# The first third of the adaLN product in two halves by output feature, with block 0 of the input projection begun on the first half; the squares of x summed along rows on ACT

## The chip, the cores and the metric

The kernel runs on one core of a Trainium2 chip. The metric is device time in microseconds (us). A core has a matrix engine (PE), a vector engine (DVE), a scalar engine (ACT), GpSimd (POOL), a sequencer that here only issues transfers (SP), and 16 DMA engines that all queues share.

## The reference, cut to what matters

One layer of a decoder trunk, for 256 prompt tokens and 8 sample tokens (264 in all, T), D = 1024, all float32:

```
mod = silu(c) @ w_ada + b_ada                  # 9 rows of c; (1024 x 6144), six parts of 1024: sh1 sc1 gt1 sh2 sc2 gt2
h   = rmsnorm(x, norm1_g) * (1 + sc1) + sh1    # x * rsqrt(mean(x*x) + eps) per token
proj = h @ w_in                                # (1024 x 9216)
...                                            # pooling and retention mixers, gates, w_out, x = x + gt1 * mix
...                                            # second modulated norm, router, top-4 of 32 experts, final norm
```

Everything in `proj` needs `h`, and `h` needs columns 0 to 2047 of `mod` (sh1 and sc1). The other 4096 columns are needed much later.

## The kernel before, in words

**Layout.** Inside the core x is held turned: `xT` and `hT` are [128 partitions, 8 chunks k of the feature, 264 tokens]. The rows of x (`xtok`, three tiles of tokens) are turned by PE, and ACT copies each chunk out of PSUM.

**Weights through a ring.** Three buffers of 2 MiB, `ring[0..2]`, take weights in the order of the list `order`: twelve loads of w_ada (`("ada", n)`) and eighteen blocks of 512 columns of w_in (`("in", p)`). SP issues a load when the last user of its buffer is done (`fetch`). The first four ada loads (`ADA_FIRST`) hold two chunks k each, of the columns 0 to 2047; the other eight hold one chunk k each of columns 2048 to 6143, and stand between the blocks of w_in. The order is ada 0 to 3, in 0, ada 4, in 1, ada 5, in 2, and so on. A buffer is used again by the third load after it.

**PE.** It turns c and x, multiplies ada 0 and 1 with c, sums the squares of x (`sum_squares`: ones times the squares that ACT writes chunk by chunk), turns the pooling state of the samples (`old_inputs_turned`), multiplies ada 2 and 3, and turns the 9 rows of sh1 and sc1 back into columns (`ada_columns(0)`). Only then can block 0 start. From there on it goes block, ada, block, ada.

**DVE and ACT.** DVE turns the sum into 1/rms for every token on all partitions (`norm`: scale, ACT's square root, a reciprocal of 128x264), multiplies `xT` by it, copies the adaLN rows out of PSUM (`stage_rows`), adds the bias (`take_columns`) and makes `scale1`. ACT then scales and shifts eight chunks of `hT` (`modulate`), and each one lets PE's first matmuls of block 0 go (`h_ready`).

**POOL** waits until all eight chunks of `hT` are done, and then loads the rest of the constants (1.96 MB) and eight rows of bias on a queue of its own. ACT loads the pooling state (`spool`, 0.48 MB) at the start on its queue.

**Later stages** are a retention stage with states streamed in and out, the up and out projections, and the experts, whose weights (32 times 12 MiB) pass through six buffers.

## Time and profile before

| | us |
|---|---|
| median of 3 runs (1546.3 to 1547.55) | 1547.12 |
| the profiled execution | 1545.43 |
| its span, first to last instruction | 1543.6 |
| PE busy | 1274.3 (83%) |
| share of PE and of DMA in the chain that ended last | 56% and 40% |
| first matmul of block 0 starts | 37.35 |
| first matmul of block 1 starts | 55.21 |

The profile shows one execution. Busy time of an engine is a sum over the program; the chain of waits follows the work that ended last, back from the end, and says of each piece whether it was an engine at work or a transfer. An arrow in a row names what the engine was waiting for. fp32 matmuls appear as two records each. "128*32" means that 32 columns of weights were loaded, so four such matmuls lie side by side in the array.

### The profile page before, as it was taken

To read this page: it belongs to the slowest core of one execution; us is meant where nothing else is said; L and a number is where in the kernel's file an instruction comes from. 1 tells how busy PE (TensorE), PEld (TensorE's weight loads), DVE (VectorE), ACT (ScalarE), POOL (GpSimd) and SP (SyncE) were. 2 spreads that over 40 slices of the span, in tenths; PEclk is the share of its full clock that TensorE was granted. 3 is DMA by queue.
4 is the path that set the end of the run, shared out by engine and by line. 5 is a ranking of instruction groups with operands and counts; after the bars stand their busy time and mean duration, and the time that the engine had idled before them with its cause. 6 is when DMAs were issued, how large, how long until landed. Compare 5 with 4: busy or idle time off the path is not lost.

```text
span 1543.6 us, 27740 instructions
## 1 busy us (share of the span) xinstructions
PE 1274.3 (83%) x10968; PEld 701.2 (45%) x10969; DVE 348.2 (23%) x747; ACT 308.1 (20%) x636; POOL 180.4 (12%) x296
## 2 busy tenths in 40 slices
PE   6999999998999889999965499576978666964594
PEld 3777887666887634444422134232433222421141
DVE  1023114332511432222211122111221112211123
ACT  3000122443100212222211022111212111211123
POOL 0240100110360001111100001000100000000000
PEclk9999999999999889999987689787989878887697
DMA  9876724999454576799999999999999999999994
GB/s 365 305 277 236 272 90 172 374 393 357 150 192 175 207 313 263 282 427 423 418 426 423 416 405 424 425 428 426 413 426 412 427 421 419 409 430 425 423 412 177
DMA packets 76666, 534.76 MB, mean 346 GB/s; under 512 B 6356, under 2 KB 7468, under 8 KB 49777
## 3 DMA queue, kind: packets, MB, share of 16 engines
q1 hardware_dynamic: 67330, 503.47, 79.7%
q0 software_dynamic: 8912, 29.90, 5.9%
q10 hardware_dynamic: 391, 0.93, 0.2%
q8 instruction: 23, 0.38, 0.1%
q14 instruction: 10, 0.08, 0.0%
HBM read 508.74 MB, written 28.09 MB: 348 GB/s over the span
## 4 chain that ended last, share of the span: by engine, by line
PE 56%; DMA 40%; DVE 2%; SPq 1%; issue 1%; ACT 0%; DVEq 0%; POOL 0%; POOLq 0%; ACTq 0%
DMA ring<-in_w_expert_in_dram 21%; PE ps L749 14%; PE ps L899 14%; PE ps L923 9%; DMA moe_ring<-in_w_expert_out_dram 8%; DMA moe_ring<-in_w_expert_in_dram 4%; DMA vslot<-in_state_ret_dram 3%; PE ps L504 2%; PE ps L868 2%; PE ps L776 2%; PE ps L822 2%; PE ps L784 2%; PE ps L791 2%; DMA ring<-in_w_ada_dram 1%; PE ps L551 1%; DMA ring<-in_w_in_dram 1%
## 5 line engine op out<-in xcount | busy, mean ns | idle before, releaser
L899 PE MATMUL ps<-ring,xgT 128*32 128x512 f32 x2352 | 323.5, 673 | 178.4 <-DMA ring<-in_w_expert_in_dram 177.7
L749 PE MATMUL ps<-hT,ring 128*128 128x264 f32 x1152 | 267.6, 390 | 3.0 <-DMA ring<-in_w_in_dram 3.0
L749 PEld LDWEIGHTS ps<-hT,ring 128*128 128x128 f32 x1152 | 218.2, 191 | 56.8 <-issue 19.5
L899 PEld LDWEIGHTS ps<-ring,xgT 128*32 128x32 f32 x2352 | 66.6, 117 | 320.1 <-DMA ring<-in_w_expert_in_dram 184.9
L923 PE MATMUL ps<-moe_ring,actT 128*32 128x256 f32 x3136 | 182.7, 381 | 3.2 <-DMA moe_ring<-in_w_expert_out_dram 2.4
L1135 ACT ACTIVATE ostage<-ps,slots_w 32x256 f32<-32x256 f32 x196 | 91.5, 467 | 288.0 <-PE ps L923 286.2
L1483 DVE COPY xg<-ps 128x256 f32<-128x256 f32 x49 | 20.8, 425 | 546.8 <-PE ps L868 546.8
L923 PEld LDWEIGHTS ps<-moe_ring,actT 128*32 128x32 f32 x3136 | 99.5, 111 | 86.6 <-issue 19.8
L899 PE MATMUL ps<-moe_ring,xgT 128*32 128x512 f32 x784 | 93.6, 595 | 19.6 <-DMA moe_ring<-in_w_expert_in_dram 19.6
L868 PE MATMUL ps<-rows,picked 128*32 128x256 f32 (+1 forms) x1200 | 81.8, 386 | 0.0
L1127 ACT COPY actT<-ps 128x256 f32<-128x256 f32 x49 | 18.3, 373 | 306.8 <-PE ps L504 306.8
L1493 DVE TENSOR_SCALAR glu_g<-ps 64x512 f32<-64x512 f32 x49 | 33.5, 683 | 178.1 <-PE ps L899 178.1
L1632 POOL CAST bias_sel<-ct 96x32 bf16 x49 | 10.4, 211 | 537.7 <-PE ps L899 294.9
L1642 POOL DMA_INDIRECT moe_rows<-ostage,slot_u x49 | 65.7, 1341 | 35.4 <-issue 34.5
L1118 ACT COPY lin<-ps 64x512 f32<-64x512 f32 x49 | 28.5, 582 | 176.8 <-PE ps L899 176.8
L899 PEld LDWEIGHTS ps<-moe_ring,xgT 128*32 128x32 f32 x784 | 23.3, 109 | 84.8 <-issue 44.0
L504 PEld LDWEIGHTS ps<-ct,act 64*128 64x128 f32 x196 | 27.2, 210 | 53.9 <-issue 53.9
L868 PEld LDWEIGHTS ps<-rows,picked 128*32 128x32 f32 (+1 forms) x1200 | 33.4, 108 | 38.5 <-issue 21.2
L1474 DVE TENSOR_SCALAR picked<-ct,item_base,rankm 128x128 f32<-128x128 f32 x147 | 42.2, 344 | 36.5 <-issue 36.5
L1637 POOL COPY slot_u<-slots_u 128x1 uint32 x49 | 9.0, 184 | 310.9 <-ACT ostage L1135 310.9
L1041 ACT ACTIVATE outer<-ps,projT 128x512 f32<-128x512 f32 x64 | 38.7, 696 | 7.8 <-DVE vslot L1354 7.8
L876 PEld LDWEIGHTS ps<-slot_v,picked 128*128 128x128 f32 x300 | 38.0, 194 | 3.2 <-issue 3.2
(276 smaller groups left out, 1112.5 us busy)
## 6 DMA issues: line engine op xcount, KB each, us to landing
ring<-in_w_expert_in_dram SPq DMA_DIRECT2D x96, 2048.0 KB, 11.9
moe_ring<-in_w_expert_out_dram SPq DMA_DIRECT2D x64, 2048.0 KB, 12.2
moe_ring<-in_w_expert_in_dram SPq DMA_DIRECT2D x32, 2048.0 KB
ring<-in_w_in_dram SPq DMA_DIRECT2D x18, 2048.0 KB, 11.7
ring<-in_w_ada_dram SPq DMA_DIRECT2D x12, 2048.0 KB, 8.7
ring<-in_state_ret_dram SPq DMA_DIRECT2D x8, 1024.0 KB, 11.1
vslot<-in_state_ret_dram SPq DMA_DIRECT2D x8, 1024.0 KB, 14.3
out_dram<-ring POOLq DMA_DIRECT2D x8, 1024.0 KB, 8.7
```

The lines of the kernel that those rows point to most:

```text
L504: return nc.tensor.transpose(out, in_, ident[0:in_.shape[0], 0:in_.shape[0]])
L749: mm = nc.tensor.matmul(ps[:, j, 0:T], ring[s][:, k, j * P:(j + 1) * P], hT[:, k, :], start=(k == 0), stop=(k == KC - 1))
L776: mm = nc.tensor.matmul(ps[:, ba, 0:T], a[:, k, m * P:(m + 1) * P], projT[:, Q0 + k, :], start=(k == 0), stop=(k == KC - 1))
L868: mm = nc.tensor.matmul(side(6, g)[:, 0:QUARTER], picked[0:n, t, 0:SLOTS], rows[0:n, t, g * QUARTER:(g + 1) * QUARTER], start=(t == 0), st ...
L876: mm = nc.tensor.matmul(ps[:, 5, 0:2], picked[:, t, :], values, start=(t == 0), stop=(t == 2))
L899: mm = nc.tensor.matmul(side(0, g), xgT[:, a, j * SLOTS:(j + 1) * SLOTS], w[:, a, g * COL:(g + 1) * COL], start=False, stop=(j == 3 and a ...
L923: mm = nc.tensor.matmul(side(2, g)[:, 0:QUARTER], actT[:, a, h * SLOTS:(h + 1) * SLOTS], w[:, a, g * QUARTER:(g + 1) * QUARTER], start=Fal ...
L1041: nc.scalar.activation(outer[:, n % 2, c, :], ps[:, 4 + n % 2, :], ACT.Copy, scale=projT[:, K0 + 2 * h + c, TP + b:TP + b + 1]).then_inc(o ...
L1135: mv = nc.scalar.activation(ostage[:, g * QUARTER:(g + 1) * QUARTER], ps[side, 2, 0:QUARTER], ACT.Copy, scale=slots_w[side, bass.ds(q, 1)])
L1474: ts(picked[:, t, :], const("slot"), item_base[:, bass.ds(q, 1)], rankm[:, t, bass.ds(e, 1)], ALU.add, ALU.is_equal).then_inc(picked_ready, 1)
L1493: ts(glu_g[:], ps[0:2 * SLOTS, 0, :], LIMIT, None, ALU.min).then_inc(glu_ready, 1)
L1642: pool.indirect_dma_start(out=moe_rows, out_offset=bass.IndirectOffsetOnAxis(ap=slot_u[0:SLOTS, 0:1], axis=0), in_=ostage[:], in_offset=No ...
```

## The change

**Halves by output feature.** The first 2048 columns of w_ada are still loaded as four pieces of 2 MiB, but a piece holds now four chunks k of half the output features: ada 0 and 1 give sh1 and sc1 for features 0 to 511 (chunks 0 to 3 of `hT`), ada 2 and 3 for features 512 to 1023. A piece comes as two transfers (one of sh1's columns, one of sc1's) with rows of 2 KB instead of 8 KB. Ada 2 and 3 no longer go into the ring but into two buffers of their own (`ada_far`), in memory that the projection fills only later, so no transfer up to ada 3 has to wait for PE. The order of issue is ada 0, ada 1, in 0, ada 2, ada 3, ada 4, in 1.

**Block 0 in two halves.** PE multiplies k = 0 to 3 of all four columns of block 0 after the first half of the adaLN columns, then ada 2 and 3, then k = 4 to 7. DVE and ACT make `hT` in the same two halves.

**Squares by rows.** ACT squares the rows of x as they came and sums along the row (`accum_out`), so the mean square is a [128, 4] column. DVE makes the 1/rms of it, three diagonal matrices of it, and PE spreads them with three matmuls of ones times the diagonal. The 16 records of matmuls on squares and the 128x264 reciprocal go. DVE copies `xT` out of PSUM in ACT's stead.

**The pooling state** is loaded by ACT after the first half of `hT`, and turned by PE after block 0.

**Else.** Three semaphores that only pace a sequencer become one (`paced`), and one unused one goes.

```diff
-        order = [("ada", n) for n in range(ADA_FIRST)]
+        order = [("ada", 0), ("ada", 1), ("in", 0)]
         for n in range(ADA_FIRST, ADA_CHUNKS):
-            order += [("in", n - ADA_FIRST), ("ada", n)]
+            order += [("ada", n)] + [("in", n - ADA_FIRST + 1)] * (n < ADA_CHUNKS - 1)
...
         def ada_source(n):
             if n < ADA_FIRST:
-                return w_ada[0].rearrange("(k p) n -> p k n", p=P)[:, 2 * n:2 * n + 2, 0:2 * D]
+                rows, cols = HALF * (n % 2), COL * (n // 2)
+                return w_ada[0, :, 0:2 * D].rearrange("(k p) (c n) -> p k c n", p=P, c=2)[:, rows:rows + HALF, :, cols:cols + COL]
...
-            for i in range(shared + 2):
+            for i in range(3):
+                fetch(i)
+            for n in range(2, ADA_FIRST):
+                for c in range(2):
+                    sp.dma_start(ada_chunk(None, n)[:, :, c, :], ada_source(n)[:, :, c, :]).then_inc(far_loaded[n - 2], 16)
+            for i in range(3, shared + 2):
                 fetch(i)
...
+            pe.wait_ge(diag_ready, 3)
+            for t, (t0, n) in enumerate(TILES):
+                mm = nc.tensor.matmul(ps[:, 6, t0:t0 + n], ones[0:n], x_diag[0:n, t, 0:n], start=True, stop=True)
+            mm.then_inc(root_spread, 1)
...
                 if kind == "ada":
                     ada_rows(at_load, p)
                     if p == 1:
-                        pe.wait_ge(vec_copied, 1)
-                        sum_squares(0)
-                        pe.wait_ge(x_copied, KC)
-                        old_inputs_turned()
-                    elif p == ADA_FIRST - 1:
-                        ada_columns(0)
...
+                        first_columns(0)
+                elif p == 0:
+                    pe.wait_ge(loaded[s], 16 * nth_of(at_load))
+                    for half in range(2):
+                        if half == 1:
+                            for n in range(2, ADA_FIRST):
+                                ada_rows(None, n)
+                            first_columns(1)
+                        pe.wait_ge(samples_ready, half + 1)
+                        for j in range(4):
+                            for k in range(HALF * half, HALF * (half + 1)):
+                                if j == 0:
+                                    pe.wait_ge(h_ready, k + 1)
+                                mm = nc.tensor.matmul(ps[:, j, 0:T], ring[s][:, k, j * P:(j + 1) * P], hT[:, k, :], start=(k == 0), stop=(k == KC - 1))
+                            if half == 1:
+                                mm.then_inc(in_ready, 1)
+                    old_inputs_turned()
...
+            for t, (t0, n) in enumerate(TILES):
+                nc.scalar.activation(x_sq[0:n], xtok[0:n, t, :], ACT.Square, accum_out=x_var[0:n, t:t + 1]).then_inc(sq_ready, 1)
+                act_e.wait_ge(sq_ready, t + 1)
+            act_e.wait_ge(var_ready, 1)
+            nc.scalar.activation(x_var[:], x_var[:], ACT.Sqrt).then_inc(std_ready, 1)
+
+            for half in range(2):
+                act_e.wait_ge(normed, half + 1)
+                for k in range(HALF * half, HALF * (half + 1)):
+                    nc.scalar.activation(hT[:, k, 0:TP], hT[:, k, 0:TP], ACT.Identity, bias=modT[:, k, 0:1],
+                                         scale=scale1[:, k, 0:1]).then_inc(h_ready, 1)
+                if half == 0:
+                    load(spool[:], state_pool[0].rearrange("b t d -> (b t) d"), spool_in)
...
+            def first_half(half):
+                k0, cols = HALF * half, slice(QUARTER * half, QUARTER * (half + 1))
+                ks = slice(k0, k0 + HALF)
+                step(tt(hT[:, ks], xT[:, ks], over(rstd[:], HALF), ALU.mult))
+                dve.wait_ge(ada_ready, 2 * half + 2)
+                cp(mod_stage[0][:, cols], ps[:, 4, cols]).then_inc(ada_staged, 1)
+                dve.wait_ge(ada_turned, half + 1)
+                turned = ps[:, ADA_TURNED[0], cols].rearrange("p (j g n) -> p g j n", j=2, g=4)[:, :, :, 0:NB]
...
```

How the instructions of PE stand from the end of the turned x to the start of block 1, before. L544 is an ada load of the first four, L526 the squares, L749 a block, L551 a later ada load; ring_59 to ring_61 are the three buffers.

```order
L504 MATMUL ps<-ct,rows_69 128x72
L544 MATMUL ps<-ring_59,cT 32x512 x8
L544 MATMUL ps<-ring_60,cT 32x512 x8
L526 MATMUL ps<-sq,ct 128x264 x8
L504 MATMUL ps<-ct,spool 128x120 x8
L544 MATMUL ps<-ring_61,cT 32x512 x8
L544 MATMUL ps<-ring_59,cT 32x512 x8
L504 MATMUL ps<-ct,mod_stage_88 128x128 x4
L749 MATMUL ps<-hT,ring_60 128x264 x32
L551 MATMUL ps<-ring_61,cT 32x512 x8
L749 MATMUL ps<-hT,ring_59 128x264 x32
```

The same stretch of PE now. L566 is an ada load of the first four, L774 half of block 0, L573 and L786 what L551 and L749 were.

```order
L523 MATMUL ps<-ct,rows_69 128x72
L566 MATMUL ps<-ring_61,cT 32x256 x16
L566 MATMUL ps<-ring_59,cT 32x256 x16
L523 MATMUL ps<-ct,mod_stage_93 128x128 x2
L774 MATMUL ps<-hT,ring_60 128x264 x16
L566 MATMUL ps<-ada_far_90,cT 32x256 x16
L566 MATMUL ps<-ada_far_91,cT 32x256 x16
L523 MATMUL ps<-ct,mod_stage_93 128x128 x2
L774 MATMUL ps<-hT,ring_60 128x264 x16
L523 MATMUL ps<-ct,spool 128x120 x8
L573 MATMUL ps<-ring_61,cT 32x512 x8
L786 MATMUL ps<-hT,ring_59 128x264 x32
```

Half of block 0 now stands ahead of the last two ada loads, the squares are gone, and the pooling state's turns have moved behind block 0.

What SP issues first, before, each row a transfer (or two):

```order
L422 DMA xtok<-in_x_sample_dram 8x1024
L405 DMA ring_59<-in_w_ada_dram 128x2x2048
L405 DMA ring_60<-in_w_ada_dram 128x2x2048
L405 DMA ring_61<-in_w_ada_dram 128x2x2048
L405 DMA ring_59<-in_w_ada_dram 128x2x2048
L407 DMA ring_60<-in_w_in_dram 128x8x512
L405 DMA ring_61<-in_w_ada_dram 128x4096
L407 DMA ring_59<-in_w_in_dram 128x8x512
```

And what SP issues first now:

```order
L436 DMA xtok<-in_x_sample_dram 8x1024
L417 DMA ring_61<-in_w_ada_dram 128x4x512 x2
L417 DMA ring_59<-in_w_ada_dram 128x4x512 x2
L421 DMA ring_60<-in_w_in_dram 128x8x512
L441 DMA ada_far_90<-in_w_ada_dram 128x4x512 x2
L441 DMA ada_far_91<-in_w_ada_dram 128x4x512 x2
L419 DMA ring_61<-in_w_ada_dram 128x4096
L421 DMA ring_59<-in_w_in_dram 128x8x512
```

Block 0's weights now come third instead of fifth, and the bytes up to the last row are the same.

## Rows read from the trace of the kernel before

**Rows 1.** Chain that ended last, 0 to 120 us: start, length, what
```profile
2.83 18.03 DMA ring<-in_w_ada_dram
...
22.89 14.21 DMA ring<-in_w_in_dram
...
53.43 1.85 PE ps L551 x16
```
**Rows 2.** Timeline of PE, 0 to 140 us: start, length, line, shape, records [idle before]
```profile
16.02 3.64 PE L544 MATMUL ps<-ring,cT 128*32 128x512 f32 x16 [1.09 <-DMA ring<-in_w_ada_dram]
20.90 1.92 PE L544 MATMUL ps<-ring,cT 128*32 128x512 f32 x16 [1.24 <-DMA ring<-in_w_ada_dram]
...
27.43 0.99 PE L504 MATMUL ps<-ct,spool 120*128 120x120 f32 x8
...
33.69 0.66 PE L504 MATMUL ps<-ct,mod_stage 128*128 128x128 f32 x4 [0.91 <-DVE mod_stage L1215]
37.35 16.08 PE L749 MATMUL ps<-hT,ring 128*128 128x264 f32 x64 [3.00 <-DMA ring<-in_w_in_dram]
...
55.21 14.51 PE L749 MATMUL ps<-hT,ring 128*128 128x264 f32 x64
```
**Rows 3.** DMA in 2 to 8 us by queue: packets, MB, share
```profile
q1 hardware_dynamic: 353, 1.51, 72.2%
```
**Rows 4.** DMA sums in 8:14, 16:21 and 58:64 us; the spool load's time to landing
```profile
DMA packets 293, 1.84 MB, mean 306 GB/s; under 512 B 16, under 2 KB 16, under 8 KB 122
...
DMA packets 274, 2.11 MB, mean 423 GB/s; under 512 B 16, under 2 KB 16, under 8 KB 16
...
DMA packets 796, 2.34 MB, mean 390 GB/s; under 512 B 16, under 2 KB 16, under 8 KB 744
...
spool<-in_state_pool_dram ACTq DMA_DIRECT2D x1, 480.0 KB, 11.6
```
**Rows 5.** Timeline of DVE and ACT, 26 to 54 us: start, length
```profile
26.84 1.28 ACT L995 ACT_TABLE_LOAD   x1
...
34.39 0.31 DVE L1225 TENSOR_TENSOR modT<-ps,vecT 128x144 f32<-128x144 f32 x1 [0.75 <-PE ps L504]
...
35.00 4.04 ACT L1001 ACTIVATE hT<-hT,modT,scale 128x256 f32<-128x256 f32 x8 [5.13 <-DVE scale L1232]
...
46.35 0.43 DVE L1238 COPY projT<-ps 128x264 f32<-128x264 f32 x1 [10.87 <-PE ps L749]
```
**Rows 6.** Chain in 505 to 640 us: the experts' matmuls of 256 columns
```profile
565.76 3.50 PE ps L923 x64
```
**Rows 7.** DMA in 43.2 to 48 us by queue; load issued at 32.84, us to landing
```profile
q0 software_dynamic: 112, 1.76, 88.0%
q1 hardware_dynamic: 154, 0.31, 17.2%
...
ring<-in_w_in_dram SPq DMA_DIRECT2D x1, 2048.0 KB, 21.8
```
**Rows 8.** Timeline of POOL from 35 us; its load's us to landing
```profile
39.36 0.72 POOL L1549 DMA_DIRECT2D ct<-in_consts_dram  x1 [38.86 <-ACT hT L1001]
...
ct<-in_consts_dram POOLq DMA_DIRECT2D x1, 1964.5 KB, 10.4
```
**Rows 9.** Stages: us, PE, PEld, DVE, ACT, POOL busy, clock, DMA, GB/s
```profile
37.35:41.00 3.65, 3.65 (x9) 2.89 (x10) 0.00 (x0) 1.69 (x4) 1.64 (x3) 0.56 0.97 400
...
53.40:167.00 113.60, 113.60 (x560) 87.37 (x560) 23.05 (x35) 5.31 (x14) 23.16 (x16) 1.00 0.70 263
...
262.00:372.00 110.00, 101.73 (x506) 69.49 (x504) 40.52 (x36) 48.25 (x92) 12.06 (x16) 0.97 1.02 383
...
1000.00:1400.00 400.00, 293.28 (x3268) 119.75 (x3268) 73.99 (x191) 72.69 (x152) 35.62 (x76) 0.86 1.00 421
```
**Rows 10.** Timeline 1526 to 1544 us: ACT's row sum over 1024 columns
```profile
1532.25 1.06 ACT L1163 ACTIVATE y_sq<-y_out 128x1024 f32<-128x1024 f32 x1 [9.26 <-DVE y_out L1515]
...
1533.21 0.19 ACT L1163 ACTIVATION_READ_ACCUMULATOR y_sq<-y_out 128x1 f32 x1
```

More of the change, by code:

```diff
@@ L42 @@
 ADA_FIRST = 4
+HALF = KC // 2
 ADA_TURNED = (7, 4, 7)
@@ L361, in slot_of, with loads_of @@
         def slot_of(i):
-            return i % RING if i < shared else 2 - i % 2
+            return (i + 2) % RING if i < shared else 2 - i % 2
+        def loads_of(i):
+            return 2 if order[i][0] == "ada" and order[i][1] < ADA_FIRST else 1
         def nth_of(i):
-            return sum(slot_of(m) == slot_of(i) for m in range(i + 1))
-        slot_loads = [sum(slot_of(m) == s for m in range(len(order))) for s in range(RING)]
+            return sum(loads_of(m) for m in range(i + 1) if slot_of(m) == slot_of(i))
+        slot_loads = [sum(loads_of(m) for m in range(len(order)) if slot_of(m) == s) for s in range(RING)]
         def spot(i):
@@ L1203, in modulate_samples, with take_x @@
-            def modulate_samples(h, scale, shift0):
-                step(tt(h[:, :, TP:T], h[:, :, TP:T], scale[:, :, 1:NB], ALU.mult))
-                tt(h[:, :, TP:T], h[:, :, TP:T], modT[:, shift0:shift0 + KC, 1:NB], ALU.add).then_inc(samples_ready, 1)
+            def take_x(first, end):
+                for k in range(first, end):
+                    dve.wait_ge(x_turned, k + 1)
+                    cp(xT[:, k, :], ps[:, k % 4, 0:T]).then_inc(x_copied, 1)
+            take_x(0, 3)
+            dve.wait_ge(sq_ready, 3)
```

180 lines of the change are left out of this document (90 added, 90 removed).

## The prediction, written before the changed kernel ran

> **What bounds the kernel now.** I read the chain of waits first, from the start to block 1. Up to 37 us it is transfers almost alone: ada 0 and 1 end it at 20.86 us, and block 0's weights, issued at 22.89 us, at 37.10 us [rows 1]. The timeline of PE shows the other side: it stands 3.00 us before block 0 for those weights [rows 2]. The DMA views say why: the engines carry 306 to 423 GB/s from 8 us on and never run dry [rows 4], so the prologue is a fixed number of bytes ahead of block 0. From 53.4 us to 167 us PE has no gap (113.60 us busy of 113.60) [rows 9]. Behind that come a stage at a DMA share of 1.02 and the experts at 1.00 [rows 9], but the transfers of both are issued when PE or a store is done. So an earlier start of block 1, at 55.21 us [rows 2], moves everything behind it, and the whole change is read as one time: when does block 1 start?
>
> **The bytes up to ada 3.** The sum needs x and c (1.12 MB), four ada pieces and block 0's weights (5 x 2.10 MB), 11.61 MB on SP's queue. By 8.0 us it has moved 1.51 MB [rows 3]; I leave that as it is. 10.10 MB remain. The pieces' rows are now 2 KB, as those of w_in are. The stretch with mostly such packets ran at 390 GB/s, the one with 8 KB packets at 423 [rows 4]; I take 400, since 390 includes a start: 25.2 us, to 33.3 us. To this comes the pooling state, 0.49 MB, still wanted before ada 3 has landed: 1.2 us. While it ran beside the ada loads the rate was 306, not 423 [rows 4], which is 6.0 x (1 - 306/423) = 1.7 us lost; beside packets of 2 KB the loss may be anything from nothing to that, and I take 0.8. Ada 3 lands at 35.3 us; bounds 33.1 (423 GB/s, which gives 23.9 us, and no loss) and 36.8 (390 GB/s, 25.9 us, and all of the loss).
>
> **What has to be done before, and is.** Of x: ACT's three row sums cost 1.25 us each [rows 10], from 8.0 to 11.8 us; then a small operation on DVE, the table load of 1.28 us [rows 5], a root, and the reciprocal and three diagonals at some 0.15 to 0.35 us each, by about 14.5 us. PE's turns of x end at 14.6 us now and wait for DVE's copies of 0.43 us [rows 5] in place of ACT's, so the diagonals cost PE about 1 us, and ada 0 starts at about 16, as before, although it has landed. Ada 0 is multiplied at the lower clock level (3.64 us against 1.92 for the same records [rows 2]) and ada 1 lands at about 18 us. Both are done by 21.5 to 23 us, `hT`'s first half 2.3 us later. Block 0's weights land at 8.0 + 5.9 MB/0.40 = 22.8 us. The first half starts at 24 to 25.5 us and takes 14.51/2 = 7.25 us, so PE is through with it and ada 2 at 33 to 35 us, before ada 3 lands. All edits on the x path (16 records of squares gone, the 128x264 reciprocal gone, ACT's copies to DVE) are thus worth nothing by themselves: ada 3's transfer covers them, with 0 to 2 us to spare. If the cover were gone, they would cost their overrun one for one.
>
> **From ada 3 to block 1.** After it has landed the chain is: 32 records of 256 columns at 3.50/64 us [rows 6], 1.75; DVE's copy of 256 columns, 0.43 [rows 5]; two turns, half of 0.66 and a start [rows 2], 0.43; two adds and the scale, where the add and the scale were 0.61 in all (34.39 to 35.00 [rows 5]), 0.85; ACT's first chunk, of which eight take 4.04 us, so 0.5 us each and a little for the first's start, 0.58 [rows 5]; the second half of block 0, 7.25; the pooling state's turns, which stood in covered time and now are on the path, 0.90 (0.99 [rows 2] less the overlap); ada 4, 1.85 [rows 1]. Sum 14.04, and 0.3 for five more semaphores: 14.3 us. 35.3 + 14.3 = 49.6 us. Two uncertain things get 0.4 us each: the clock, and the tail of block 1's weights (both below). Block 1 starts at 50.4 us, 4.8 us earlier than before.
>
> It holds a gain that isn't about bytes: before, the granted clock was 0.56 from 37.35 to 41.00 us [rows 9], and block 0 took 16.08 us where every later one took 14.51 [rows 2], 1.57 us lost behind the 3.00 us of idling. Now PE has work in that time.
>
> **Everything else.** One semaphore for three and one increment less: nothing. Stores, states and experts are issued relative to PE, so they shift. Profiled execution: 1545.43 - 4.8 = 1540.6 us. Its median stood 1.7 us above it (1547.12), so the median should be 1542.3 us.
>
> **Rivals.**
>
> *The clock falls in the new gap.* PE idles 1 to 2 us before ada 3 and again briefly while DVE and ACT finish `hT`. For: 3.00 us of idling brought the low level before [rows 2, 9]. Against: the gaps of 1.09 and 1.24 us ahead of ada 0 and 1 were not followed by a slower stretch, 1.92 us being the good figure [rows 2]. Price: ada 3's matmuls 3.64 for 1.92, and 1.57 on the half block, 3.3 us, of which 0.4 is in the sum: 1545.2 us. The Trainium skill (TensorE: Matmul & The Clock Gate, section "Part 1: The HAM clock gate") says that the throttled state is the default and activity releases it, so that a pause costs more than its own length. By that rule the trace agrees, with 16.08 us for 14.51; a kernel that cuts one wait into two would be at risk twice.
>
> *Block 1's weights come late.* They are last in SP's queue. Before, POOL's load of 1.96 MB, issued at 39.36 us [rows 8], got in between: from 43.2 to 48 us POOL's queue moved 1.76 MB and SP's 0.31 [rows 7], and the transfer issued at 32.84 us took 21.8 us, to 54.6, only 0.6 us ahead of block 1. So this wait is next in line. Now: ada 4 lands 5.0 us after ada 3 and block 1's weights 5.3 later, at ada 3 + 10.3. POOL waits for the eighth chunk, at ada 3 + 5.5, and its bytes came 3.8 us after issue, so at about ada 3 + 9.6. The last 0.7 us of SP's transfer run beside it at a fifth or less of the rate, and end at + 12.6 to + 14.5, where block 1 needs them at + 14.3. If POOL's data come 1 us earlier, or SP's 1 us later, block 1 waits for them until POOL's load is over, about ada 3 + 5.8 + 10.4 = 51.5 us, or until the eight bias rows are, some 54 us. Price 1.5 to 4 us of the gain: 1545.0 us. The Trainium skill (DMA: Bandwidth & Descriptors, section "Queues, rings and completion order") says that each engine goes round its queues packet by packet. The trace agrees: 112 packets of 16 KB beside 154 of 2 KB [rows 7]. It speaks against this change, since it makes the pieces' packets small on SP's queue, and the pooling state's are not.
>
> *Small packets make the loads slow; this one ends slower.* If the ada pieces in rows of 2 KB, two transfers each, ran at the 306 GB/s of the mixed stretch [rows 4] and not at 400, the 10.10 MB would take 33.0 us instead of 25.2: 7.8 us later, block 1 at 58.2 us, the median at 1550.1. It decides below 10.1/(25.2 + 4.8) = 337 GB/s. For: four times as many packets for the same bytes in the one stretch that bounds the prologue. Against: w_in has those rows today, and runs at 390 [rows 4].
>
> *The gain is given back.* The state stage and the experts are bound by transfers at a share of 1.02 and 1.00 [rows 9], so a head start could end in a wait for them: 1547.1 us. For: nothing in the chain but those shares. Against: no transfer there has a time of its own to start; each waits for PE or a store.
>
> **How the numbers follow.** Forecast 0.60, with 1540.3 to 1544.3 us as its own range (a gain of 6.8 us, where ada 3 lands at 34 us, before which PE isn't ready for it, and both allowances go unused; and of 2.8, ada 3 at 36.8 with both used up and 0.5 more on the x path). The clock 0.13, late weights 0.15, slow packets 0.04, given back 0.08. 0.2% is 3.1 us, about what a measurement tells from no change. Faster by more: 0.9 of the forecast (0.54), 0.3 of the clock and late-weight cases (0.08), and a little of a better one where no allowance is used (0.02): 0.64. Slower by more: slow packets, half of them, and the worst end of late weights together with a late ada 3: 0.05. The rest within. Range 1540.0 to 1547.0: below it 0.06, above it 0.12.
>
> **What would show it.** Right: no wait of SP up to ada 3; ada 3 landing at 33 to 37 us; PE idle before it, and then 14 us to block 1 with no wait for `ring`; a granted clock of 1.00 from 25 us on; block 1 at 49 to 52 us; the distance from there to the end within 1 us of the 1488.4 us of before (1543.6 - 55.21). Wrong: PE at work when ada 3 lands (then the x path or the clock bound the prologue), a wait for w_in before block 1, less than 340 GB/s in 10 to 30 us, or a distance to the end that grew.

## The result

The changed kernel takes 1551.18 us (median of 9 runs, 1549.81 to 1553.36) against 1547.12 (9 runs, 1543.8 to 1549.52) beside it: ratio 1.0029, interval 1.0019 to 1.0039. By the ratio it is 4.5 us slower (the medians differ by 4.1); 4.8 us faster was forecast, a median of 1542.3 in a range of 1540.0 to 1547.0. The profiled execution took 1549.95 us, span 1548.1, so 4.5 us more than that of before. Of all executions reported here three (1757.0 and 2182.02 us in e13, 6949.64 in e14) were far slower than the rest of their kernel and are left out of its ratio. Where the 4.5 us arose, by the two traces:

| us | before | after | more |
|---|---|---|---|
| start of block 1 | 55.21 | 56.00 | 0.8 |
| block 1 to the first state load into `vslot` | 202.39 | 202.39 | 0 |
| from there to the second load of w_up_pool ("state stage") | 143.5 | 145.1 | 1.6 |
| from there to the load of w_out | 45.4 | 45.4 | 0 |
| load of w_out to the first expert load, in which PE multiplies the up projection | 42.72 | 44.81 | 2.1 |
| experts to the end | 1054.4 | 1054.5 | 0.1 |

The first row is within the scatter of unchanged kernels: in the second trace of before block 1 starts at 56.20 us, and in six runs that leave the prologue alone (e13 to e18) between 55.04 and 57.08.

### The profile page after: what moved, and what is told of

Its sections match the earlier page's. It is cut to its first block, busy times and chain, and to the rows that moved or that the text cites. A ratio compares the mean times of both kernels' runs of the same rounds, so it can differ in the third digit from the quotient of the medians.

```text
span 1548.1 us, 27874 instructions
## 1 busy us (share of the span) xinstructions
PE 1273.4 (82%) x11022; PEld 702.0 (45%) x11023; DVE 352.6 (23%) x768; ACT 305.4 (20%) x626; POOL 180.4 (12%) x296
## 4 chain that ended last, share of the span: by engine, by line
PE 54%; DMA 39%; SPq 2%; DVE 2%; issue 1%; ACT 1%; DVEq 0%; ACTq 0%; POOL 0%; POOLq 0%
DMA ring<-in_w_expert_in_dram 23%; PE ps L786 14%; PE ps L936 13%; DMA moe_ring<-in_w_expert_out_dram 10%; PE ps L960 10%; PE ps L523 2%; DMA vslot<-in_state_ret_dram 2%; PE ps L905 2%; PE ps L859 2%; DMA moe_ring<-in_w_expert_in_dram 2%; PE ps L813 2%; PE ps L828 2%; PE ps L821 2%; DMA ada_far<-in_w_ada_dram 1%; PE ps L573 1%; PE ps L660 1%
## 5 line engine op out<-in xcount | busy, mean ns | idle before, releaser
L786 PE MATMUL ps<-hT,ring 128*128 128x264 f32 x1088 | 251.5, 388 | 0.0
L786 PEld LDWEIGHTS ps<-hT,ring 128*128 128x128 f32 x1088 | 205.1, 190 | 50.8 <-issue 16.8
## 6 DMA issues: line engine op xcount, KB each, us to landing
ring<-in_w_in_dram SPq DMA_DIRECT2D x18, 2048.0 KB, 11.4
```

Of the source, the lines that this page charges most:

```text
L786: mm = nc.tensor.matmul(ps[:, j, 0:T], ring[s][:, k, j * P:(j + 1) * P], hT[:, k, :], start=(k == 0), stop=(k == KC - 1))
```

## The profile after

PE's timeline of the changed kernel from its start, columns as in [rows 2], which it answers:

```profile
14.49 1.74 PE L541 MATMUL ps<-x_diag,ct 128*128 128x128 f32 x6
...
16.48 5.96 PE L566 MATMUL ps<-ring,cT 128*32 128x256 f32 x64
...
25.14 7.44 PE L774 MATMUL ps<-hT,ring 128*128 128x264 f32 x32 [1.64 <-ACT hT L1032]
32.70 1.93 PE L566 MATMUL ps<-ada_far,cT 128*32 128x256 f32 x32
38.10 3.56 PE L566 MATMUL ps<-ada_far,cT 128*32 128x256 f32 x32 [3.47 <-DMA ada_far<-in_w_ada_dram]
42.26 0.44 PE L523 MATMUL ps<-ct,mod_stage 128*128 128x128 f32 x2 [0.60 <-DVE mod_stage L1264]
44.35 9.05 PE L774 MATMUL ps<-hT,ring 128*128 128x264 f32 x32 [1.65 <-ACT hT L1032]
53.23 0.99 PE L523 MATMUL ps<-ct,spool 120*128 120x120 f32 x8
54.15 1.92 PE L573 MATMUL ps<-ring,cT 128*32 128x512 f32 x16
```

PE reaches ada 3 early, as forecast, and then stands 3.47 us for it. Behind that gap the same 32 records that took 1.93 us for ada 2 take 3.56, and the second half of block 0 takes 9.05 us where the first took 7.44. The windows of the changed kernel (columns of [rows 9]) give the clock:

```profile
32.60:34.70 2.10, 1.93 (x32) 0.93 (x32) 0.00 (x0) 0.00 (x0) 0.00 (x0) 1.00 1.06 389
38.06:41.70 3.64, 3.56 (x32) 1.46 (x32) 0.00 (x0) 0.00 (x0) 0.00 (x0) 0.53 0.94 391
44.30:53.30 9.00, 8.95 (x33) 7.27 (x34) 0.43 (x1) 2.14 (x5) 4.70 (x9) 0.81 0.89 335
53.40:167.00 113.60, 113.60 (x564) 87.31 (x563) 23.05 (x35) 6.71 (x22) 23.38 (x17) 1.00 0.71 266
```

It is at 2.4 GHz (1.00) for ada 2, near 1.2 (0.53) for all of ada 3, and at a mean of 0.81 over the half block. The DMA view in 8 to 14 us, in 25 to 31 us, and of queue 1 up to ada 3's landing at 38.06 us [rows 3, 4]:

```profile
DMA packets 1167, 2.32 MB, mean 387 GB/s; under 512 B 32, under 2 KB 32, under 8 KB 1167
...
DMA packets 891, 1.99 MB, mean 331 GB/s; under 512 B 41, under 2 KB 41, under 8 KB 891
...
q1 hardware_dynamic: 5625, 12.51, 90.6%
```

With 2 KB rows alone the engines carry 387 GB/s, and 331 with the pooling state beside them. When ada 3 had landed, SP's queue had moved 12.51 MB, although the bytes up to and with ada 3 are 11.61: it had already moved 0.90 MB of the loads behind. Last, the chain of waits after, start, length, what:

```profile
20.32 17.74 DMA ada_far<-in_w_ada_dram
...
445.27 12.43 DMA vslot<-in_w_up_ret_dram
...
457.75 3.83 PE ps L828 x16
```

The first piece answers to [rows 1]. The second was not in the chain of before: PE now stands 1.83 us for a load of the up projection, some 400 us behind the start of block 1.

## Experiments on the prologue

**Both kernels again**, unchanged (e1_again the changed one, e2_before_again the one before): 1552.46 us, ratio 1.0035 (1.0022 to 1.0048), and 1547.41, ratio 1.001 (0.9998 to 1.0022). The loss comes again. In the second trace of the changed kernel the state stage is 146.6 us and the up stage 47.2; in that of before 144.8 and 42.72.

> The changed kernel once more, for a second trace and a tighter ratio. In its first trace block 1 starts at 56.00 us, 0.8 later than before (55.21), but the span is 4.5 longer: 1.6 more are lost in the stage of the states and 2.1 in the up projection, where PE waits for a w_up_ret load. Theory A (the loss is the prologue's and the rest is spread of the races between queues): block 1 again near 56, the downstream distance (1492.1 then, 1488.4 before) moves by some us from run to run, and need not be 1492 again; median 1548 to 1552. Theory B (something behind the prologue is slower for a reason that the change brings): the distance from block 1 to the end is again 1491 to 1493, and the wait in the up projection is there again.

> The kernel before, unchanged, for a second trace of it. Ratio 1.000 within 0.002. Theory A: the distance from the start of block 1 to the end differs from 1488.4 us by some us in this trace (1487 to 1492), so that one pair of traces says little on it. Theory B: 1488 to 1489 again, with no wait in the up projection.

**PE kept busy (e3_busy).** Matmuls whose result nobody reads fill the gaps around ada 3.

```diff
+            def keep_busy(count):
+                for i in range(count):
+                    nc.tensor.matmul(ps[:, 6, 0:256], ones, ct[:, 0:256], start=True, stop=True)
...
-                            for n in range(2, ADA_FIRST):
-                                ada_rows(None, n)
+                            ada_rows(None, 2)
+                            keep_busy(7)
+                            ada_rows(None, 3)
                             first_columns(1)
+                            keep_busy(3)
```

> The changed kernel with 7 matmuls of 256 columns put between ada 2 and ada 3 on PE, and 3 behind the turns of the second half, that write a bank nobody reads; they fill the 3.47 and 1.65 us in which PE idled there. Clock theory (the gap made the granted clock fall, which cost 3.56 - 1.93 = 1.6 us on ada 3's matmuls and 9.05 - 7.25 = 1.8 us on the half block): ada 3's matmuls take 1.9 us, the half block 7.3, block 1 starts at 52.6 us, 3.4 earlier, and the median falls by 3.4 us, to 1547.8. Rival (the prologue's time doesn't come through to the end, or the half block was slow for its own pace by ACT's chunks): block 1 at 55 to 56 us, or at 52.6 with a median over 1550.

PE's timeline in that run:

```profile
34.83 3.29 PE L586 MATMUL ps<-ct 128*128 128x256 f32 x14
38.35 1.93 PE L566 MATMUL ps<-ada_far,cT 128*32 128x256 f32 x32 [0.24 <-DMA ada_far<-in_w_ada_dram]
...
43.00 7.44 PE L780 MATMUL ps<-hT,ring 128*128 128x264 f32 x32 [0.35 <-ACT hT L1038]
...
53.04 14.51 PE L792 MATMUL ps<-hT,ring 128*128 128x264 f32 x64
```

Ada 3 landed no earlier, but its matmuls take 1.93 us again and the half block 7.44. Block 1 starts at 53.04, 3.0 us earlier than in the changed kernel, close to the clock rival's price of 3.3 us. The median is 1546.98, ratio 1.0004 (0.9993 to 1.0015): level with before, not faster, though block 1 starts 2.2 us earlier than in [rows 2].

**The pooling state's load later (e4_spool_late)**, behind the second half of `hT`.

```diff
-                if half == 0:
+                if half == 1:
                     load(spool[:], state_pool[0].rearrange("b t d -> (b t) d"), spool_in)
```

> The changed kernel with the load of the pooling state issued behind the second half of hT instead of the first, so that it no longer runs beside the loads that ada 3 waits for. Theory (it cost ada 3 its own 1.2 us and 1.7 us by mixing: the rate was 331 GB/s in 25 to 31 us and 387 before): ada 3 lands at 35.2 us instead of 38.06, the gap before it shrinks from 3.5 to 0.6 us so that the clock stays up, and block 1 starts at 49.5 to 50.5; median 1545 to 1546. Rival 1 (the bytes are what counts, not the mixing, and the clock falls all the same): ada 3 at 36.9, block 1 at 54.5 to 55. Rival 2 (block 1's weights or the pooling state now come late, behind POOL's 1.96 MB): ada 3 early, but a wait for ring or spool before block 1 and a gain under 2 us.

```profile
26.45 8.94 PE L774 MATMUL ps<-hT,ring 128*128 128x264 f32 x32 [1.64 <-ACT hT L1032]
35.32 3.66 PE L566 MATMUL ps<-ada_far,cT 128*32 128x256 f32 x64
...
52.11 14.51 PE L786 MATMUL ps<-hT,ring 128*128 128x264 f32 x64
```

Ada 3 lands at 36.52 us, 1.5 earlier (35.2 was expected, 36.9 by the first rival). In PE's timeline the wait for it is gone, and ada 2 and 3 run without a break. Block 1 starts at 52.11 us, although now the first half took 8.94 us for 7.44, behind the same 1.64 us of idling. The median is 1551.2 all the same, ratio 1.0028 (1.0014 to 1.0041): 3.9 us won before block 1 and none at the end.

**The same in the kernel before (e7_before_spool_late)**: the load behind `modulate`, its turns behind block 0, in other PSUM banks.

```diff
-            load(spool[:], state_pool[0].rearrange("b t d -> (b t) d"), spool_in)
...
             modulate(hT, scale1, 0, 1)
+            load(spool[:], state_pool[0].rearrange("b t d -> (b t) d"), spool_in)
...
+                    if p == 0:
+                        old_inputs_turned()
```

> One part of the change alone on the kernel before: the pooling state is loaded behind the modulation of hT and turned after block 0; ada thirds, ring order and squares as before. In the prologue it gives the loads ahead of block 0 1.2 us for its bytes and up to 1.7 us of mixing: block 0's weights land at 34.2 to 35.9 us instead of 37.1, block 0 starts at 35.6 to 36.0 (hT's first chunk is ready at 35.6), the gap before it shrinks from 3.0 to 1.3 us so that the clock stays up (block 0 in 14.6 us instead of 16.1), and with 0.9 for the turns block 1 starts at 53.0 instead of 55.2 to 56.2. Theory that the prologue's time comes through to the end: median 1544 to 1545. Theory that stages behind it turn on more than that: any median from 1543 to 1549, with a distance from block 1 that differs from 1488.4 to 1489.9.

Block 0 starts at 34.12 us instead of 37.35 but takes 17.49 (clock 0.83 from 34.1 to 51.6 us), behind idle times of 2.00 and 1.80 us. Block 1 starts at 54.36; ratio 0.9996 (0.9977 to 1.0014).

**Both cures (e8_best)**: e4 with three fillers of e3 behind each pair of turns.

> The changed kernel with the late pooling state and three filler matmuls before each half of block 0. With the late load alone the first half ran at the low clock (8.94 us) and PE was only just through when ada 3 had landed. Here the first half takes 7.4 us, block 1 starts at 50.5 to 51.5 us (52.1 with the late load alone). If block 1's start comes through, the median is 1.0 to 1.5 us under that one's 1551.2; if the stages behind it decide, it is anything from 1545 to 1552.

```profile
40.47 7.44 PE L781 MATMUL ps<-hT,ring 128*128 128x264 f32 x32 [0.35 <-ACT hT L1039]
...
54.05 16.19 PE L793 MATMUL ps<-hT,ring 128*128 128x264 f32 x64 [2.77 <-DMA ring<-in_w_in_dram]
```

Ada 3 lands at 35.78 us. With PE that early the late-weights rival comes true: PE's timeline has 2.77 us of waiting for block 1's weights, and the block behind it takes 16.19 us for 14.51. Ratio 1.003 (1.0012 to 1.0048).

## Experiments on what lies behind block 1

PE has the same 10763 records from block 1 on in both kernels. What differs is how many stand ahead: 10968 records in all before, 11022 matmul records and as many weight loads after, so 108 instructions more. PE's instructions come in fetches of 16 KB (queue 8, one packet each), and these fall at other moments: before at 210 and 235 us behind block 1's start, after at 221 and 246 (the expectations below say 209 and 233 for the first two, since they were read from views of 2 us each). SP's loads of states in [block 1 + 215 to 255 us], start, time from the first of two issues to the end of the second, before:

```profile
274.16 6.18 SPq L414 DMA_DIRECT2D ring<-in_state_ret_dram  x2
...
297.77 5.90 SPq L414 DMA_DIRECT2D ring<-in_state_ret_dram  x2
```

and after:

```profile
274.95 7.20 SPq L428 DMA_DIRECT2D ring<-in_state_ret_dram  x2
...
298.56 7.55 SPq L428 DMA_DIRECT2D ring<-in_state_ret_dram  x2
```

Both first issues stand at block 1 + 219, but the second waits for the store of the slot, which was issued at block 1 + 215. The DMA views of before (269.7 to 272.2 us) and after (270.5 to 273, and 275 to 278) show the store, us to landing, and the fetch:

```profile
out_dram<-ring POOLq DMA_DIRECT2D x1, 1024.0 KB, 9.6
```
```profile
out_dram<-ring POOLq DMA_DIRECT2D x1, 1024.0 KB, 10.6
...
q8 instruction: 1, 0.02, 2.0%
```

It is the first difference that is handed on: the store lands 1.0 us later, the next load is issued that much later, and load, update, store and load hand it on.

**What a fetch does to a transfer.** The store of 256 KB that is issued at block 1 + 193.8 has the DMA engines to itself. It consists of 64 packets of data and 16 closing ones of 4 bytes, one for each engine's share. The DMA view of before (247.9 to 251 us) has them all:

```profile
DMA packets 80, 0.26 MB, mean 85 GB/s; under 512 B 16, under 2 KB 16, under 8 KB 80
...
out_dram<-s_stage POOLq DMA_DIRECT2D x1, 256.0 KB, 2.3
```

In the changed kernel a fetch starts 0.8 us behind the issue. The views of 248.7 to 251.72 us and of 251.72 to 252.72:

```profile
DMA packets 77, 0.27 MB, mean 88 GB/s; under 512 B 15, under 2 KB 15, under 8 KB 76
...
q8 instruction: 1, 0.02, 1.9%
...
out_dram<-s_stage POOLq DMA_DIRECT2D x1, 256.0 KB, 3.2
...
DMA packets 4, 0.01 MB, mean 12 GB/s; under 512 B 1, under 2 KB 1, under 8 KB 4
```

Fifteen closing packets come in time; the last, and three packets of data before it, come in the next microsecond. So the fetch's packet (1.9% of 16 engines' 3.02 us, 0.92 us) holds up one share of the sixteen, and the store lands with its last share. All traces agree: this store took 3.2 to 4.0 us in the five where a fetch starts 0.8 to 1.6 us behind its issue (after, e1, e4, e5, e9), and 2.3 in the other fifteen. For the busy store at + 215 it looks the same: before, its closing packets come by block 1 + 224.4; after, fifteen by + 224.3 and the last at + 225.35.

**Counts moved by semaphore increments (e5, e6).** e5_before_shifted is the kernel before with 108 increments on PE (and 21 on DVE, as many as the change adds there); e6_after_shifted the changed one with 148 on PE and 235 on DVE. With the change's own 108 that is 256 on PE, a whole fetch (the trace has 24 for 23), which puts the fetches back.

```diff
+            for i in range(108):
+                pe.sem_inc(pe_pace, 1)
             pe.wait_ge(const_in, 16)
...
+            for i in range(21):
+                dve.sem_inc(pe_pace, 1)
             dve.wait_ge(c_turned, 1)
```

> The kernel before, with 108 increments of a semaphore that nobody waits for at the start of PE's program and 21 at the start of DVE's, where both idle. That puts as many more instructions ahead of block 1 as the change does. In two traces of before the instruction fetches (queue q8, 16 KB each) come 209 and 233 us after block 1's start, in two traces of the changed kernel 221 and 246; and the state stage is 143.5 and 144.8 us long before, 145.1 and 146.6 changed, the distance from block 1 to the end 1488.4 and 1489.9, and 1492.1 and 1495.5. Fetch theory (the shifted fetches make a late transfer later in stages where load, update and store wait for each other): fetches at 221 and 246, the distance 1492 or more, the median 4 to 5 us over before, 1551. Rival (the number of instructions has nothing to do with it, the downstream loss has another cause): the fetches move, distance 1488 to 1490, median 1546 to 1548.

> The changed kernel with 148 such increments on PE and 235 on DVE, in stretches where both idle, so that with the change's own 108 and 21 the count is 256 up and the fetches should fall where they fell before. Fetch theory: fetches near 209 and 233 us after block 1, distance to the end 1488 to 1490, block 1 at 56, median 4 us under the changed kernel's, 1547.5 to 1548.5. Rival: distance 1492 to 1496, median 1551 to 1553.

The increments cost time of their own, so block 1 starts at 62.48 and 72.00 us, and the ratios, 1.0088 (1.0061 to 1.0114) and 1.0097 (1.0075 to 1.0118), say little by themselves. Less block 1's delay against [rows 2] (7.3 and 16.8 us), e5 loses 6.3 us more and e6 nothing, each give or take 4 us. SP's rows of e5 and of e6:

```profile
281.43 7.41 SPq L415 DMA_DIRECT2D ring<-in_state_ret_dram  x2
...
305.03 7.25 SPq L415 DMA_DIRECT2D ring<-in_state_ret_dram  x2
```
```profile
290.95 6.18 SPq L429 DMA_DIRECT2D ring<-in_state_ret_dram  x2
...
314.55 6.17 SPq L429 DMA_DIRECT2D ring<-in_state_ret_dram  x2
```

The kernel before, with the changed one's count, has the changed one's pairs, and waits 1.55 us for w_up_ret; the changed one, with the fetches put back, has the pairs of the one before and no wait.

**Small matmuls in place of increments (e9, e10), DVE alone (e11), the changed kernel busy and put back (e12).** e9_before_pe108 adds 27 matmuls of 8 columns (108 instructions) to the kernel before, e10_before_pe52 adds 13, e11_before_dve21 only the 21 DVE increments. e12_after_busy_phase is e3 with 29 small ones and five fillers for seven.

```diff
+            def tiny(count):
+                for i in range(count):
+                    nc.tensor.matmul(ps[:, 5, 0:8], ones, ct[:, 0:8], start=True, stop=True)
...
+            tiny(8)
             pe.wait_ge(x_in, 32)
...
+                    if p == 0:
+                        tiny(8)
...
                         ada_columns(0)
+                        tiny(11)
```

> The kernel before with 27 matmuls of 8 columns (108 instructions on PE, 54 loads of weights and 54 matmuls, as many as the change adds) put where PE idles in the prologue: 8 behind the turns of c, 8 between ada 0 and 1, 11 ahead of block 0. Their results aren't read. The increments of the run before took some 0.15 us each and moved the whole prologue by 7 us; these cost nothing there, and may keep the clock up for block 0 (1.6 us). Fetch theory (PE's instruction fetches, not the length of the prologue): fetches at 221 and 246 us after block 1, state stage 145.1 us or more (before: 143.5, 144.8), a wait in the up projection likely, and a median of 1548 to 1550, over before by 3 to 5 less 1.6. Rival (number of PE's instructions without effect): 143.5 to 144.8 and no wait, median 1545 to 1546.5.

> The same with 13 such matmuls, 52 instructions, half the shift: fetches near 215 and 240. The fetch theory has no forecast for which phase is good; it allows a third value of the state stage and of the median. The rival says as before, 143.5 to 144.8 and 1545.5 to 1547.5.

> The kernel before with only the 21 increments at the start of DVE's program, which idles there until 6.97 us. If it is PE's fetches that matter, this is as before: block 1 at 55.2 to 56.2, state stage 143.5 to 144.8, no wait in the up projection, ratio 1.000 within 0.0015. If it is DVE's, it is like the changed kernel behind block 1: 145 or more, median 1550.

> The changed kernel with fillers in PE's gaps as in the third experiment, and 27 more matmuls of 8 columns, so that PE has 256 instructions more than before ahead of block 1 and its fetches fall as before (209 and 233). Block 1 at 53.0. Fetch theory: state stage 143.5 to 144.8, no wait in the up projection, distance 1488 to 1491, median 1543 to 1545, faster than both kernels. Rival: as the third experiment, 1547, state stage 146.

| | PE more | fetches, us from block 1 | block 1 | second pair | wait w_up_ret | ratio (interval) |
|---|---|---|---|---|---|---|
| e9 | 108 | 222, 247 | 56.34 | 7.53 | 0.91 | 1.0048 (1.0033 to 1.0064) |
| e10 | 52 | 229 | 55.23 | 6.59 | 0 | 1.0005 (0.999 to 1.0021) |
| e11 | 0 | 211, 234 | 54.64 | 5.97 | 0 | 1.0006 (0.9996 to 1.0017) |
| e12 | 256 | 210, 235 | 55.69 | 5.61 | 0 | 1.0002 (0.9988 to 1.0015) |

e9 is the changed kernel's loss without the change: 7.4 us by the ratio, 1.1 of them ahead of block 1. e12 is the reverse: block 1 starts within 0.3 us of the changed kernel's, and the median, 1547.72, is 3.5 us below its 1551.18 (4.2 by the two ratios). Over e1 to e12 and the two first traces, the second pair took 7.25 to 7.60 us in the seven with fetches at 219 to 223 and 245 to 247 (after, e1, e3, e4, e5, e8, e9), and 5.61 to 6.59 in the seven without. PE waits for w_up_ret in five of the seven (not in e3 and e8) and in none of the others. The state stage took 145.1 to 147.3 us in the seven and 143.5 to 145.1 elsewhere; e12, with 145.05, missed its expected 143.5 to 144.8 and is no shorter there than the changed kernel's first trace.

**Is it the fetch's packet?** e13 to e18 leave PE alone and let ACT copy 16 KB at two moments: e13, e15 and e17 at those of the changed kernel's fetches, e14, e16 and e18 some 7 and 11 us later.

```diff
                         if i < KC:
                             take_mixed(i)
+                        if i in (2, 6):                      # e13, e15, e17; (3, 7) in the others
+                            r = (2, 6).index(i)
+                            nc.scalar.dma_start(scrap[r:r + 1], w_in[0, r:r + 1, 0:4096]).then_inc(spool_in, 16)   # e13, e14
+                            nc.scalar.dma_start(scrap[r:r + 1], ct[64:65, 0:4096]).then_inc(spool_in, 16)          # e15, e16
+                            nc.scalar.dma_start(scrap[16 * r:16 * r + 16], ct[64:80, 0:4096]).then_inc(spool_in, 16)  # e17, e18
```

> The kernel before, with two single transfers of 16 KB (one row of w_in into a scratch row that nothing reads) issued by ACT at about 218.8 and 242.4 us behind block 1's start, so that their packet falls where the instruction fetches of the changed kernel fall (219 to 222 and 245 us) and where this kernel has none of its own. PE's instructions are untouched. Theory (a packet of 16 KB on one DMA engine holds up the store of the state's slot that lies on it by about 1 us, and the loop of load, update, store and load carries it on): the store issued at block 1 + 215 lands after 10.6 us or more, not 9.6; SP's two state loads behind it stand 7.2 to 7.6 us apart in all, not 6.2, and the next two 7.3 or more, not 5.9; the state stage takes 145 us or more instead of 143.5, a wait of 1 to 4 us for w_up_ret appears, and the median is 2 to 5 us above before's. Rival (the fetch itself, that is PE's sequencer, or chance, and not the packet): store 9.6 us, pairs 6.2 and 5.9, no wait, the median that of before.

> The same two packets, issued at about 225.7 and 254 us behind block 1's start, so at about 227 and 256, where neither kernel's fetches hurt (228 and 252 in the run with 52 instructions more, which was as fast as before). Theory: store 9.6 us, SP's pairs 6.2 and 5.9 to 6.6, no wait for w_up_ret, the median within 1.5 us of before's. Rival (any two packets more cost this much, or the moment doesn't matter): the same loss as in the run with the packets at 219 and 243.

> As the run with two small transfers at block 1 + 217 and + 241 us, whose 16 KB the chip split into 32 packets of 512 bytes, spread over the engines, and which changed nothing (pair of state loads 6.10 and 5.72 us, store 9.5 us). Now the 16 KB are one row of the constants written to a scratch row, which should be one packet on one engine, as an instruction fetch is. Theory (one long packet on one DMA engine holds up the store's slice on it by its own 1 us): store 10.4 us or more, pairs 7.2 to 7.6 and 7.3 or more, a wait for w_up_ret of 1 us or more, the median 2 to 5 us above before's. Rival (a packet does not do it; the fetch marks something else): 9.6, 6.2, 5.9, none, the median of before.

> The same two one-row transfers at block 1 + 225 and + 253 us. Theory: the first store is untouched (9.6 us, pair 6.2), the second pair 5.9 to 6.6, no wait, the median within 1.5 us of before's. Rival (the moment doesn't matter): as the run with the rows at + 217 and + 241.

> As the run with one row of 16 KB at block 1 + 217 and + 241 us, which moved the store's landing by only 0.2 us (9.8 us; pairs 6.35 and 5.81) and left the median where it was. Now sixteen such rows in each of the two transfers, one for each DMA engine, 0.5 MB in all. Theory left (the delay counts only on the engine whose part of the store ends last, which one packet on some other engine doesn't touch): with every engine held up by 1 us the store lands after 10.4 us or more, the pairs take 7.2 us or more, a wait for w_up_ret appears, and the median is 2 to 6 us above before's, more than the 1.2 us that 0.5 MB cost at 420 GB/s. Rival (the stage forgives a microsecond of DMA time at that moment, and the loss with the instruction fetch has another way): the median at most 1.5 us above before's, no wait.

> The same sixteen rows twice, at block 1 + 225 and + 253 us. Theory left: the first pair 6.2 to 6.5, the median at most 1.5 us above before's (the bytes alone). If it loses as much as the run with the rows at + 217 and + 241, then DMA time costs the same wherever in this stage it falls, and the moment of a fetch explains nothing.

In e13 and e14 the 16 KB went as 16 packets of 1 KB and 16 closing ones (not as 32 of 512 bytes, as e15's expectation has it). In e15 it is one packet, as a fetch is; the DMA view at block 1 + 220 to 222, and SP's rows:

```profile
q10 hardware_dynamic: 1, 0.02, 1.9%
...
273.99 6.35 SPq L415 DMA_DIRECT2D ring<-in_state_ret_dram  x2
...
297.59 5.81 SPq L415 DMA_DIRECT2D ring<-in_state_ret_dram  x2
```

In e17 sixteen such packets come at once:

```profile
q10 hardware_dynamic: 20, 0.26, 32.8%
...
275.17 6.62 SPq L415 DMA_DIRECT2D ring<-in_state_ret_dram  x2
...
298.77 6.98 SPq L415 DMA_DIRECT2D ring<-in_state_ret_dram  x2
```

| | store lands after | second pair | ratio (interval) |
|---|---|---|---|
| e13, e14 (small packets) | 9.5, 9.6 | 5.72, 6.00 | 1.001 (0.9994 to 1.0025), 0.9999 (0.9991 to 1.0008) |
| e15, e16 (one packet) | 9.8, 9.8 | 5.81, 6.26 | 0.9999 (0.9987 to 1.0011), 1.0011 (1.0001 to 1.0022) |
| e17, e18 (sixteen) | 10.0, 9.4 | 6.98, 5.55 | 1.0014 (1.0005 to 1.0024), 1.0015 (1.0004 to 1.0025) |

None of the six brings back the loss or a wait for w_up_ret, and by the medians the two moments cost the same (e17 2.2 us, e18 2.3). In e17 the store, the pairs and the missing wait fell short of its theory. This does not clear the fetch's packet. ACT's single packet took 0.61 us (1.9% of 16 engines' 2 us), a fetch's 0.92 to 1.3, and the shares of the busy store end anywhere between + 223.6 and + 224.4 in the kernel before, so a short hold-up of one share need not show; which engine a packet is on, the trace doesn't say. One does show as a fetch would: in e16 ACT's packet starts at + 227.5, and of the store issued at + 220.0 fifteen closing packets come by + 228.4 and the last at + 229.3. With sixteen packets (e17) that store took 11.4 us where before's took 9.0, and the second pair's 6.98 is above all traces without the changed kernel's fetches.

Put together: the place of PE's fetches decides the loss behind block 1 (e5, e9; e6, e12), and the traces show the way, one share of a transfer held up by a fetch. That a copied packet alone could bring the loss is not shown, and since all fetches move together, neither is how much each of them costs.

## Why the prediction was wrong

**Ada 3's landing: mis-sized, 38.06 us for 35.3, outside the bounds of 33.1 to 36.8.** The queue had moved 1.58 MB by 8.0 us (1.51 assumed). The 10.03 MB left take 25.9 us at 387 GB/s and not 25.2 (0.7 us). The pooling state lost 6.0 x (1 - 331/387) = 0.9 us by mixing, as sized (0.8), and its bytes 1.2. That makes 36.0. Without it beside them ada 3 landed 1.5 us earlier in e4 and 2.3 in e8, which is of the size of the two terms' 2.1 us. The rest, 2.1 us, is what I had no term for: I treated the queue as one pipe, but a load has landed when the last of its 16 shares has, and the other engines had gone on by 0.90 MB (2.3 us at 387 GB/s). Half of it follows a fetch of PE's instructions at 22.5 us. The views of 22 to 23, 35.9 to 36.6 and 36.6 to 37.7 us show the fetch, 14 closing packets, and the last:

```profile
q8 instruction: 1, 0.02, 6.9%
...
DMA packets 94, 0.39 MB, mean 562 GB/s; under 512 B 14, under 2 KB 14, under 8 KB 78
...
DMA packets 40, 0.48 MB, mean 438 GB/s; under 512 B 1, under 2 KB 1, under 8 KB 12
```

The last closing packet of ada 1, ahead of the fetch, comes 0.04 us behind the fifteenth; that of block 0's weights 1.04 us behind it, and that of ada 3, at 37.57 us, 1.07. As I read it, the engine that carried the fetch had no idle time in which to catch up. In sixteen of the twenty traces the lag of the last share so grows from at most 0.28 us to 0.65 or more behind the first fetch; in e4, e8 and e16 one share was 0.8 to 1.0 us late ahead of it, for a reason not shown, and in e5 it stays at 0.14. The other half of the 2.1 us I can't place. The trace of before could have told me: 0.08 us at the landing at 30.8, and 0.97 at the one at 37.10, behind a fetch at 30.7, with 12.52 MB moved by then for 11.61 due. The same error put block 0's weights at 24.85 us for 22.8, barely ahead of the first half (25.14).

**From ada 3 to block 1: 17.9 us for 14.3.** Ada 3's records took 3.56 (term 1.75) and the half block 9.05 (7.25), 3.6 us together, of which 0.4 was allowed; the copy, turns, adds and ACT's first chunk came as sized. This is the clock rival, given 0.13. I argued from gaps of 1.09 and 1.24 us that had cost nothing, for a gap that I put at 1 to 2 us; it became 3.47 because ada 3 was late, so the first error fed the second. e3 shows the price. The Trainium skill (TensorE: Matmul & The Clock Gate, section "HAM oscillation — how this bites in real kernels") says that a wait for a transfer between groups of matmuls lets the engine start the next one throttled. The trace agrees: 3.56 us for 1.93 behind 3.47 us of waiting. Short gaps are not safe either: in e4 and e7 idle times of 1.6 to 2.0 us stood ahead of slow stretches (8.94 for 7.44; 17.49 for 14.51). Yet the 1.64 us ahead of the first half in the changed kernel, as long as e4's, were followed by 7.44; what tells the two apart is not shown.

Both together: 2.8 + 3.6 less the two allowances of 0.4 is 5.6 us, and block 1 started at 56.00 for 50.4. These are 5.6 of the 9.3 us between forecast and result; 3.7 arose behind block 1.

**"Stores, states and experts are issued relative to PE, so they shift": the step that failed.** I gave the distance from block 1 to the end as 1488.4 us within 1; it was 1492.1, and 1495.5 in the second trace. The issues do shift; their landings don't, since two kernels with equal instructions behind block 1 still differ in when PE's fetches fall. An earlier block 1 did not bring its gain to the end: with it at 53.04 (e3) the median was 1546.98, and with it at 52.11 (e4) 1551.2. I had written of a "distance to the end that grew" only as a sign of being wrong. The rival "gain given back" named the right stage and the wrong reason: there was no gain to give back.

Of the up stage the traces show how 1.6 us become 3.7. POOL's stores of cleared rows are paced by POOL's own casts, not by PE; before, they were issued at 449.44 us, 6.6 behind the load of w_up_ret at 442.88, after at 450.80, 5.5 behind that at 445.27, and the load took 12.4 us for 9.6. But nearness is not the cause: with the stores 5.85 to 5.95 us behind it the load took 9.4 to 10.0 us in e6, e12 and e15, and 11.5 and 12.2 in e9 and e5; with 5.5 in e8 it took 10.1. The five traces in which PE waits are those in which a fetch starts 0.1 to 2.6 us ahead of the load's issue. Its 16 closing packets before (451.5 to 452.1 us), and fifteen of them after (453.8 to 454.75):

```profile
DMA packets 131, 0.24 MB, mean 393 GB/s; under 512 B 16, under 2 KB 16, under 8 KB 131
...
DMA packets 161, 0.30 MB, mean 315 GB/s; under 512 B 15, under 2 KB 15, under 8 KB 161
```

The last came at 457.36 us. That the fetch held up that share by its 1 us and the stores, whose packets begin to move in that time, by the rest, is argued, not shown.

**What was right:** the x path (diagonals' matmuls at 14.49 us, table load at 11.70), the first half at 25.14 us, PE done with ada 2 before ada 3 landed, no wait for block 1's weights in the changed kernel, and that wait as next in line (e8). The missing wait was partly luck: the weights landed at 48.27 us, 10.2 behind ada 3 and not 12.6 to 14.5, since POOL issued its load 7.9 us behind ada 3, and not 5.5.

**Open.** Why ACT's single packets so seldom show as a fetch does. The Trainium skill (DMA: Bandwidth & Descriptors, section "Queues, rings and completion order") says that the semaphore write of a transfer lands only after all earlier writes of that DMA engine, on whichever queue. By that rule a fetch could hold up a store whose data are already there; in the store that had the engines to itself three packets of data were late as well, so there the rule isn't needed, and no run tests it elsewhere. Open too is why the experts' stage took 1050.9 to 1060.3 us over the traces with the same instructions: it blurs single executions (e3's was 1551.57 at a median of 1546.98), and so verdicts rest on medians. And by their medians e4 was slower at the end than its block 1 and stages explain by some 3 us, e8 by some 1 us.

## What to carry to other kernels

A head start is worth only what arrives at the end. Follow it through the next loop in which load, update and store wait for each other, and compare the distance to the end over two traces of each kernel. When an edit changes how many instructions an engine runs early, test the count by itself (instructions without effect in the kernel before) ahead of crediting or blaming the edit. When one wait is cut into several, price each for the clock too, and let the last piece's transfer land by its slowest DMA engine, not by the mean rate.

## What the runs showed of the hardware

- A fetch of PE's instructions is a packet of 16 KB that takes 0.92 to 1.3 us here and holds up one of a transfer's 16 shares. A store alone on the engines landed 0.9 to 1.7 us later for it, and the last share of a load in a full queue came some 1.0 us later.
- A semaphore increment costs PE's sequencer 0.15 us: 100 of them put the first matmul at 16.26 us, 108 at 17.49.
- 27 matmuls of 8 columns (54 records) took 8.4 us in e9, 0.16 us a record: they are no cheap filler.
- SP's issue is held back when loads pile up. Its row for the four loads of ada 2 and 3, in the changed kernel, with nothing in the program to wait for:

```profile
9.66 14.10 SPq L441 DMA_DIRECT2D ada_far<-in_w_ada_dram  x4
```

The DMA engines had work all the while, so it cost nothing here, but the next loads left SP only at 23.80 us.
